# First feed-forward block cut into slices of 256 channels, its modulation turned into columns

## Reference

```
c_act = silu(c)                                        # 1024 values
mod   = c_act @ w_ada[l] + b_ada[l]                    # 1024 x 9216 weights: shift, scale, gate of three sub-blocks
h     = rms_norm(x, norm_gain) * (1 + scale) + shift   # x: 256 x 1024
x     = x + 0.5 * gate * ((silu(h @ w_gate) * (h @ w_up)) @ w_down)     # d_ff = 2816
```

## Time and profile before

| | us |
|---|---|
| median of 3 runs | 2643.42 (2641.47 to 2643.69) |
| the profiled execution, its own time | 2643.91 |
| span of its trace | 2642.1 |
| PE, DVE, ACT busy | 2614.3, 2027.2, 1338.6 |
| DMA | 634.17 MB, mean 240 GB/s |

### The profile page before, as it was taken

One profiled execution on the slowest core, in us unless ns is written; L12 is line 12 of the kernel. 1 busy time (PEld: TensorE's weight loads), 2 busy tenths in 40 slices (PEclk: granted clock), 3 DMA queues, 4 the chain that ended last, 5 costly groups with the idle time before them and its releaser, 6 DMA issues.

```text
span 2642.1 us, 33396 instructions
## 1 busy us (share of the span) xinstructions
PE 2614.3 (99%) x13499; PEld 2184.4 (83%) x13499; DVE 2027.2 (77%) x2314; ACT 1338.6 (51%) x1514; POOL 0.8 (0%) x6
## 2 busy tenths in 40 slices
PE   7999999999999999999999999999999999999998
PEld 4888877888888877888888899888888889997887
DVE  6878888878777888877877767777787786867844
ACT  3445566544445566544544534555454454456543
POOL 0000000000000000000000000000000000000000
PEclk9999999999999999999999999999999999999999
DMA  8986855777776864688687758548768767774752
GB/s 303 321 283 224 285 202 176 257 272 251 269 272 223 297 235 154 231 279 283 222 289 265 262 195 278 186 140 294 266 212 284 266 228 258 237 239 131 249 199 85
DMA packets 316450, 634.17 MB, mean 240 GB/s; under 512 B 12419, under 2 KB 76099, under 8 KB 316297
## 3 DMA queue, kind: packets, MB, share of 16 engines
q1 hardware_dynamic: 303760, 620.78, 68.4%
q10 hardware_dynamic: 12536, 11.25, 1.5%
HBM read 630.88 MB, written 8.97 MB: 242 GB/s over the span
## 4 chain that ended last, share of the span: by engine, by line
PE 94%; DVE 4%; issue 1%; DMA 1%; ACT 0%; SPq 0%; DVEq 0%; ACTq 0%
PE bank L1581 21%; PE bank L1583 20%; PE bank L1582 20%; PE acc L1581 9%; PE acc L1583 9%; PE acc L1582 8%; PE bank L1719 1%; PE bank L1642 1%; DVE w_both L1048 1%; PE bank L1890 1%; DVE softmax L1283 1%; DMA x<-in_x 1%; PE acc L1812 0%; PE bank L1665 0%; PE acc L1872 0%
## 5 line engine op out<-in xcount | busy, mean ns | idle before, releaser
L1048 DVE TENSOR_TENSOR w_both<-raw,w_both 128x2048 fp32r<-128x2048 f32 x412 | 942.0, 2289 | 413.9 <-ACT w_both L607 413.4
L607 ACT ACTIVATE w_both<-raw 128x2048 fp32r<-128x2048 f32 x412 | 786.7, 1913 | 479.4 <-PE bank L1583 314.3
L1581 PE MATMUL bank<-w_both,h 128*128 128x512 f32 x1888 | 750.5, 398 | 2.0 <-DVE h L1154 2.0
L1583 PE MATMUL bank<-w_both,h 128*128 128x512 f32 x1888 | 736.7, 390 | 0.0
L1582 PE MATMUL bank<-w_both,h 128*128 128x512 f32 x1888 | 735.9, 390 | 0.0
L1581 PEld LDWEIGHTS bank<-w_both,h 128*128 128x128 f32 x1888 | 355.0, 188 | 76.5 <-issue 3.7
L1583 PEld LDWEIGHTS bank<-w_both,h 128*128 128x128 f32 x1888 | 354.8, 188 | 75.3
L1582 PEld LDWEIGHTS bank<-w_both,h 128*128 128x128 f32 x1888 | 355.4, 188 | 70.5 <-issue 1.0
L1092 DVE SCALAR_TENSOR_TENSOR ada_sum<-raw,c_act,ada_sum 128x512 f32<-128x512 f32 x476 | 357.5, 751 | 16.5 <-DMA raw<-in_w_ada_all 2.4
L1581 PE MATMUL acc<-w_both,y 128*128 128x512 f32 x896 | 353.3, 394 | 0.0
L1583 PE MATMUL acc<-w_both,y 128*128 128x512 f32 x896 | 349.4, 390 | 0.0
(11 more groups left out here) (219 smaller groups left out, 2393.9 us busy)
## 6 DMA issues: line engine op xcount, KB each, us to landing
raw<-in_w_ada_all SPq DMA_DIRECT2D x136, 1024.0 KB, 5.2
raw<-in_w_in SPq DMA_DIRECT2D x128, 1024.0 KB, 5.4
raw<-in_ffn_down_all SPq DMA_DIRECT2D x88, 1024.0 KB, 5.1
raw<-in_ffn_gate_all SPq DMA_DIRECT2D x80, 1024.0 KB, 5.1
raw<-in_ffn_up_all SPq DMA_DIRECT2D x80, 1024.0 KB, 5.9
raw<-in_ffn_side_all SPq DMA_DIRECT2D x16, 1024.0 KB, 5.2
raw<-in_w_branch SPq DMA_DIRECT2D x12, 1024.0 KB, 7.1
first_w<-in_w_ada_all SPq DMA_DIRECT2D x8, 1024.0 KB, 14.4
```

Source lines behind the costliest of these rows:

```text
L607: activate(halves_of[n][0], src, ACT.Copy).then_inc(high_ready.sem, 1)
L1048: tensor(halves_of[n][1], raw_of("unit", s, k, 0)[0], halves_of[n][0].bitcast(F32), ALU.subtract).then_inc(low_ready.sem, 1)
L1581: mm(dst, a_h, b_h, start=start, stop=False, skip_group_check=True)
L1583: return mm(dst, a_l, b_h, start=False, stop=True, skip_group_check=True)
```

## The change

The first block goes by slices of 256 channels instead of halves of 512. Slice q has the quarter `first_w[q]` (256 shift columns beside 256 scale columns, repacked so that each partition reads one contiguous run) and unit q (gate and up columns for those 256 rows side by side, `ffn_first`), each slice loaded in turn right behind x.

- The norm makes x times rstd alone (`tensor_scalar`), and the transposes turn that, into `turned_x`: channels in the partitions. There shift and gain * (1 + scale) are one number for each partition, and one `tensor_scalar` for each 128 x 256 tile makes h from `turned_x` (`first_slice`), in place. ACT then makes `h_high`, DVE `h_low`, tile by tile.
- So the modulation is wanted as columns. For quarter 0: tiles 0 to 3 by `first_direct`, 4 to 7 summed by DVE, row sums as before, ACT copies one partition (`first_copy`), four products with one row and one column turn it (`first_turns`). For quarters 1 to 3 (`first_by_column`): DVE sums tiles 0 to 6 of the quarter; TensorE makes four one-column products from tile 7 and `c_act`, and, once the sum is there, four one-column products from the sum and a column of ones.
- Bias and gain of the first sub-block come with the parameter rows (104 instead of 80) as columns; the gains spread over partitions and the bias rows are no longer loaded for stage 0; `c_act` is no longer copied 128 times.
- TensorE gets 4 products of zeros and 3 of constants at the start, and one (`keep_busy`) in each slice.
- `first_block` is six products for each of four groups (gate, up, two token tiles) in each slice, with the modulation of the next slice behind them.

```diff
+            for q in range(4):
+                load(q)
+                first_load(q)
             for m, (what, s, k, part) in enumerate(items):
-                if m >= 2:
+                if m >= 4:
                     load(m)
...
-                    act.wait_ge(first_done.sem, 2 if k < 4 else 4)
+                    act.wait_ge(first_turned.sem, k - 1)
...
+            first_highs(0)
+            for q in range(1, 4):
+                high(0, q)
+                first_highs(q)
+            high(0, 4)
+            high(0, 5)
...
+            def first_slice(q):
+                dve.wait_ge(first_turned.sem, q + 1)
+                linked(tensor(first_mod[:, q], first_columns(q).rearrange("p (a t) -> p a t", a=2),
+                              first_bias[:, :, 2 * q:2 * q + 2], ALU.add))
+                linked(tensor(first_mod[:, q, 1, :], first_mod[:, q, 1, :],
+                              first_params[:, 16 + 2 * q:18 + 2 * q], ALU.mult))
...
+                for i in range(2):
+                    tile = turned_x[:, 2 * q + i, :]
+                    nc.vector.tensor_scalar(tile, tile, first_mod[:, q, 1, i:i + 1], first_mod[:, q, 0, i:i + 1],
+                                            ALU.mult, ALU.add).then_inc(first_made.sem, 1)
+                for tile in (2 * q, 2 * q + 1):
+                    dve.wait_ge(first_high.sem, tile + 1)
+                    tensor(h_low[:, tile, :], turned_x[:, tile, :], h_high[:, tile, :].bitcast(F32), ALU.subtract
+                           ).then_inc(first_h.sem, 1)
...
+            for tt in range(TT):
+                if tt:
+                    first_sum(0, range(4, 8))
+                spread(0, tt)
...
+            low(0, 0)
+            first_slice(0)
+            for q in range(1, 4):
+                first_sum(q, range(7))
+                low(0, q)
+                first_slice(q)
+            low(0, 4, with_sums=False)
+            low(0, 5)
...
+            def first_by_column(q, steps):
+
+                pe.wait_ge(first_landed[q][1].sem, 16)
+                for j in range(4):
+                    mm(first_columns(q)[:, j:j + 1], first_w[:, q, 7, P * j:P * j + P], c_act[:, 0, 7:8],
+                       start=j == 0, stop=False, skip_group_check=True)
+                pe.wait_ge(first_part.sem, steps)
+                for j in range(4):
+                    last = mm(first_columns(q)[:, j:j + 1], first_w[:, q, 0, P * j:P * j + P], ones[:, 0:1],
+                              start=False, stop=j == 3, skip_group_check=True)
+                last.then_inc(first_turned.sem, 1)
+
+            def keep_busy(count):
+                for _ in range(count):
+                    mm(acc[:, 0:512], ident, const[:, 0:512], start=True, stop=True)
...
+                    for q in range(3):
+                        for tt in range(TT):
+                            first_group(q, tt, 0)
+                            first_group(q, tt, 1)
+                        keep_busy(1)
+                        first_by_column(q + 1, 4 + 7 * (q + 1))
+                    first_group(3, 0, 0)
+                    first_group(3, 0, 1)
+                    first_group(3, 1, 0)
                     turn_hidden(0, 0)
-                    up(0, 1, 1)
+                    first_group(3, 1, 1)
...
+            pe.wait_ge(zeros_ready.sem, 2)
+            for _ in range(4):
+                mm(bank[0][:, :], seed[:, 0:P], seed[:, :], start=True, stop=True)
```

More of the change, by code:

```diff
@@ L438, in unit_source @@
         def unit_source(s, k):
-            if s == 0:
-                k = {1: 2, 2: 1}.get(k, k)
+            if s == 0 and k < 4:
+                return t["ffn_first"][k], 2
             layer, l = s // 3, (s // 3) % 2
@@ L687, in silu @@
                     else:
[L688 removed]
+                        wait_used(s, UP[n] - 1 if s or n else 3)
                     if n:
@@ L705, in ffn @@
                         high_of_h(s, 1, half)
[L706 to L709, removed]
+                    high(s, 4)
+                    silu(0, 1)
+                    high(s, 5)
+                    high_of_hidden(0, 0)
+                else:
+                    high_of_hidden(0, 0)
+                    silu(0, 1)
                 high(s, 6)
@@ L989, in _, with first_highs, first_copy @@
                 activate(g, g, ACT.Copy, scale=HEAD ** -0.5).then_inc(c_ready.sem, 1)
[L990 to L993, removed]
+            def first_highs(q):
+                for tile in (2 * q, 2 * q + 1):
+                    act.wait_ge(first_made.sem, tile + 1)
+                    activate(h_high[:, tile, :], turned_x[:, tile, :], ACT.Copy).then_inc(first_high.sem, 1)
+            def first_copy(q):
+                act.wait_ge(first_done.sem, q + 1)
+                activate(first_row(q), first_acc(q)[0:1, :], ACT.Copy).then_inc(first_row_ready.sem, 1)
             root_table()
@@ L997, in _ @@
                 norm(0, tt)
-            shift_out(0)
             high(0, 0)
-            high_of_h(0, 0, 0)
-            high_of_h(0, 1, 0)
-            high(0, 1)
+            first_copy(0)
+            for half in range(2):
+                act.wait_ge(h_turned.sem, h_turned.at(0, h_count(0, 1, half)))
+                activate(turned_x[:, 4 * half:4 * half + 4, tokens(1)], fours(turn_bank(0, 1, half)), ACT.Copy
+                         ).then_inc(x_turned_act.sem, 1)
             act.wait_ge(table_ready.sem, 2)
@@ L1210, in ffn @@
                 product(0, 0)
-                low(s, 4)
                 if s == 0:
+                    sums(s, 4)
                     product(0, 1)
                     low_of_hidden(0, 0)
-                    low(s, 5)
                     low(s, 6)
@@ L1220, in ffn @@
                 else:
+                    low(s, 4)
                     low(s, 5)
@@ L1528, in _ @@
             dve.wait_ge(params_turned.sem, 1)
+            nc.vector.tensor_copy(first_params, acc[:, PARAMS:ROWS])
             nc.vector.tensor_copy(params[:, :], acc[:, 0:PARAMS]).then_inc(params_ready.sem, 1)
             dve.wait_ge(c_ready.sem, 1)
[L1531 to L1551, removed]
+            dve.wait_ge(params_ready.sem, 1)
+            linked(nc.vector.tensor_scalar(first_params[:, 8:16], first_params[:, 8:16], 1.0, None, ALU.add))
@@ L1557, in _ @@
                    ).then_inc(table_ready.sem, 1)
[L1558 to L1568, removed]
+            dve.wait_ge(zeros_ready.sem, 2)
+            for tt in range(TT):
+                if tt:
+                    first_sum(0, range(4, 8))
+                spread(0, tt)
+                for half in range(2):
+                    nc.vector.tensor_scalar(half_of(work, tt, half), half_of(x, tt, half), rstd[:, tt:tt + 1], None,
+                                            ALU.mult).then_inc(normed.sem, 1)
+            for half in range(2):
+                dve.wait_ge(h_turned.sem, h_turned.at(0, h_count(0, 0, half)))
+                nc.vector.tensor_copy(turned_x[:, 4 * half:4 * half + 4, tokens(0)], fours(turn_bank(0, 0, half))
+                                      ).then_inc(x_turned_dve.sem, 1)
+            low(0, 0)
[6 more added lines that the diff above has]
+            low(0, 5)
             for s, kind in enumerate(STAGES):
@@ L2146, in _ @@
                ).then_inc(params_turned.sem, 1)
[L2147 to L2159, removed]
+            pe.wait_ge(c_ready.sem, 1)
+            first_direct(0, range(4))
+            for half in range(2):
+                turn_h(0, 0, half)
+            first_summed(0, 4, 4)
+            for half in range(2):
+                turn_h(0, 1, half)
+            first_turns(0)
+            for half in range(2):
+                pe.wait_ge(x_turned_act.sem, half + 1)
+                pe.wait_ge(x_turned_dve.sem, half + 1)
             for s, kind in enumerate(STAGES):
@@ L2216 @@
         "rel_rows": np.ascontiguousarray(a["rel_bias"].reshape(16, REL)[:, ::-1]),
-        "rows": row(qk_gains, a["pool_scale"], a["conv_w_2"], a["c"], a["c_2"]),
+        "rows": row(qk_gains, a["pool_scale"], a["conv_w_2"], a["c"], a["c_2"], a["b_ada"][0, 0:2 * D],
+                    a["norm_gain"].reshape(6, D)[0]),
+        "first_w": a["w_ada"][0, :, 0:2 * D].reshape(8, P, 2, 4, S).transpose(3, 1, 0, 2, 4).reshape(4, P, 8, 512).copy(),
+        "ffn_first": np.stack([a[n].reshape(-1, D, D_FF)[0, :, 0:512] for n in ("ffn_w_gate", "ffn_w_up")], 1
+                              ).reshape(4, 2, P, 1024).transpose(0, 2, 1, 3).copy(),
         "bias_ada": np.concatenate([a["b_ada"], a["ada_b_2"]]),
```

102 lines of the change are left out of this document (54 added, 48 removed).

## The result

| | before | after |
|---|---|---|
| median of 11 runs each, us | 2643.48 (2641.47 to 2644.29) | 2649.63 (2645.12 to 2650.96) |
| profiled execution, its span | 2643.91, 2642.1 | 2648.6, 2646.8 |
| ratio to before, 95% interval | | 1.0023 (1.0016 to 1.0031) |

The account below looks back on a forecast made before the run. TensorE's work and waits bound the kernel, its chain setting the slices: 26.1 + 2.4 + 3 x 10.1 + 1.6 + 8.85 = 69.25 against 63.2, +6.0 us, giving 2649.4 (chance 0.42). Range 2643.5 to 2654.5.

Parts of the forecast that it names:

- The mark: End of the first block, 63.2 us before; forecast at 69.25, +6.0 us.
- The frame: PE is busy 99% of the span; whatever happens to the first 63 us moves the end by just as much.
- The first product: Start of slice 0 after loads, sums, norm and turning: 26.1 us, between 25 and 27.5, against 34.0 before.
- TensorE's chain: Per slice: 24 products 5.5, constants 0.87, one-column products 2.0, wait 1.75; sum 10.1 us, above DVE's 9.6 and DMA's 8.0.
- The clock: Half clock in slice 0 for 5.1 us, costing 2.4; one further priced fall between slices, 1.6.
- rival 1: Columns cost as forecast but the clock holds: +2.0, 2645.5; with slice 0 alone at half, 2647.9; chance 0.36.
- rival 3: Clock falls in every gap and the columns themselves run at half: 2653 to 2656; chance 0.10.
- The end of the block: Behind slice 3, turning of the first hidden tile waits for DVE's product; the block ends at H3 + 8.85.
- H3: Time of the first product of slice 3, the last slice of the first block.
- 2.9 us of idle TensorE: Behind 18 products of slice 3, TensorE waits for DVE's product before turning hidden tile 0; some 3 us as a sign.
- Rival 2: Not slower: DVE's chain, 9.6 us a slice, decides in place of TensorE's; 2642.9 to 2644; chance 0.11.
- Rival 4: The idea pays in full: DMA stays the bound at 8.0 us a slice, block end at 58; chance 0.01.

Follow-up runs that it names:

- the kernel with packed loads: Kernel before with only the DRAM layout of its first twelve 1 MB loads changed, one contiguous run per partition: 2642.26 us, ratio 0.9998.
- fill with silu early: Changed kernel, two products of constants in the wait for h replacing the one ahead of the columns, unit 5 behind silu(0, 0): 2645.40 us, ratio 1.0009.
- the warm start: Two fp32 products of constants behind the four turning products: on the changed kernel 2647.92 us; added to fill with silu early 2641.64 us, ratio 0.9998.
- fill and warm start: Changed kernel with two products of constants in each wait for h and two behind the turning products, block end unchanged: 2643.09 us, ratio 1.0000.
- fill alone: Changed kernel with the product of constants ahead of the one-column products replaced by two behind them, in the wait for h: 2644.11 us, ratio 1.0006.

## Why the prediction was right, step by step

The forecast was 2649.4 and slower; it is 2649.63. The mark it was built on, the end of the first block, was forecast at 69.25 and lies at 68.05 (the last six products from 66.61 on) in the profile of after, which is 1 us below its median. That the time was met within 0.2 us is partly luck. The block ended 1.2 us earlier than forecast in the profile, chiefly because of the first product, and the median run is 1 us slower than the profiled one. Its mean clock is 0.996 against 0.995 there, so the clock does not say by what.

- **The frame holds.** Everything behind the block moved by the same amount, and no stall appeared behind it (4.85 us at the second turn, 4.7 in the span).
- **The first product, 26.1 forecast, 24.69 found.** The term that was off is DMA. I priced 1 MB at 2.67 us from loads in runs of 2 KB; packed, they come at 422 GB/s in 20 to 30 us, where before had 387. The second half of quarter 0 was there at 15.1 instead of 16.2. From there the chain took 9.6 instead of 9.9:

```profile
15.11 0.48 DVE L1530 TENSOR_SCALAR first_w<-first_w,c_act 128x512 f32<-128x512 f32 x1 [0.77 <-DMA first_w<-in_first_w]
```

- **TensorE's chain, 10.1 forecast, 10.17 found** in the one slice at full clock: products 5.57, constants 0.86, columns 0.80 + 1.03, then 1.9 until h. The one-column products cost 0.20 each, nearly the 0.22 of those with 8 columns, so 1.8 for the eight with the end of the last, where I took 2.0; the wait was 0.15 longer than I took. The Trainium skill ("TensorE: Matmul & The Clock Gate", section "LDWEIGHTS (loading the stationary operand)") has a load of P columns of weights cost P / 1.2 ns, which is 107 ns for 128; the trace has 0.10 us for each of the two passes, close to it and a little below. That the load is what sets this cost no run shows. DVE's wait for the columns in that slice was 0.72, forecast 0.5. Fewer sums on DVE brought nothing, a shorter chain of TensorE brought 2.4 us, and the filled wait made the distance 9.36, so both ends of this step were shown.
- **The clock.** Forecast: slice 0 at half for 5.1 us (2.4 lost), found 6 us (12.94 - 10.17 = 2.8). The price was about right, but not the reason: the clock was not low from a sparse start, it was at 1.00 in 18 to 22 us and fell in the last wait, 2.90 us, which two products could fill. One fall in slices 1 and 2, forecast at 1.6; found one in slice 1 (11.70 - 10.17 = 1.5) and, in slice 3, one that cost nothing because the wait for DVE's product covered it: the turn came at 66.20, DVE's product had ended at 66.14. Which slices are hit differs by run: the runs of after go from 2645.1 (clock 0.998) to 2651.0 (0.994). By its time the former is rival 1, and the latter is on the way to rival 3; neither was profiled. Read so, forecast and rival 1 were not two mechanisms but two outcomes of one.
- **The end of the block, H3 + 8.85 forecast, 8.55 found.** The 2.9 us of idle TensorE that I listed as a sign did not show in this profile, since slice 3 ran at half clock, but a wait of 2.3 to 2.4 us is there in the four profiles with this end of the block whose slice 3 ran at full clock. What the step missed: taking that wait away alone only moves it to the next turn, whose product stands behind four sums.
- **Rival 2** is not what after does, but what it does once the wait is filled. **Rival 4** is out: nothing was being loaded in 44 to 46 us, and DVE began the sums of quarter 3 at 49.44 without a wait for it.

## What to carry to other kernels

When a block is cut into finer slices to start earlier, write down each engine's chain for one slice, with the hand-overs; the earlier start (here 9.3 us) is lost if the longest chain (10.2 us a slice, three times) exceeds what the next engine would need (9.4) and what the data would allow (an estimate of 7.5, from 3 MB at the 422 GB/s of the trace). A wait of TensorE can have two prices, its length and the half clock behind it; products of constants belong inside the wait, not ahead of it, where they lengthen the chain. And before a wait is removed, look at what is queued in front of the next thing that is waited for.

## What the runs showed of the hardware

- **A gap of the same length brings the clock down in one profile and not in the next.** TensorE's wait of 1.98 us in before was followed by a granted clock of 0.50, a wait of 2.02 in the same place of the kernel with packed loads was not. Waits of 1.98 and 1.95 us ahead of the second turn did and did not (fill with silu early, without and with the warm start), and so did waits of 2.34 and 2.35 ahead of the first (fill and warm start, fill alone).
- **fp32 products of constants in the wait kept the clock up.** The five profiles without them have 15 gaps between slices (one-column products, then 1.9 us idle); the clock fell in or just behind 11. The five with two such products in the wait have 15 gaps, and it fell in none. Ahead of slice 0 it fell, in the wait or just behind it, in all six profiles with 2.90 us open, and in none of the four with two products there, though these left up to 1.0 us open.
- **Layout in DRAM is worth 9% of the load rate** for 1 MB loads: 387 GB/s in 20 to 30 us with 2 KB runs, 422 with one contiguous run of 8 KB for each partition. In the kernel before, this gained nothing. There a load on the other queue came later (11.2 instead of 9.6 us), which would account for it.
